# Gate products of a routed expert layer: float32, or split into a rounded part and a rest

## The reference

```
eidx = take_along_axis(cidx, pos)                 # which experts, 8 heads x 16
gate = softmax(top_sc)                            # and their gates
act  = gelu(einsum('thkd,td->thk', u_tab[eb], hb))
y    = einsum('thk,thkd->td', gb * act, v_tab[eb])
```

## Time and profile before

| | us |
|---|---|
| median of 3 runs | 3418.14 (3417.44 to 3432.96) |
| the profiled execution | 3415.01 |
| its span in the profile | 3413.2 |
| PE busy | 3213.3 (94%) |
| DVE busy | 2236.4 (66%) |
| POOL busy | 1723.1 (50%) |
| ACT busy | 1360.5 (40%) |

### The profile page before, as it was taken

The page is one execution under the profiler, slowest core; times in us unless marked ns, Lnnn a source line. Parts: engine busy times, 40 slices in busy tenths (PEclk is TensorE's granted clock), DMA queues, the critical chain, the costliest instruction groups (busy, mean ns, idle before and its releaser), DMA issues.

```text
span 3413.2 us, 46478 instructions
## 1 busy us (share of the span) xinstructions
PE 3213.3 (94%) x16195; PEld 2774.4 (81%) x16195; DVE 2236.4 (66%) x4113; ACT 1360.5 (40%) x1999; POOL 1723.1 (50%) x922
## 2 busy tenths in 40 slices
PE   6999999989999999979999999898999999899998
PEld 4787787779999999979999998756888886478886
DVE  5787898769968677646666645286854332857553
ACT  4555432333454544434444443365322223632221
POOL 2222343434767667657787754662444443034443
PEclk8999999999999999989999999999999999999999
DMA  5434422223689797999999953211222232122222
GB/s 208 156 119 162 150 93 80 93 86 112 209 294 333 249 338 247 325 346 337 343 350 356 335 181 108 85 54 48 94 98 99 95 107 102 48 68 99 98 94 87
DMA packets 190046, 587.55 MB, mean 172 GB/s; under 512 B 19585, under 2 KB 52737, under 8 KB 189601
## 3 DMA queue, kind: packets, MB, share of 16 engines
q1 hardware_dynamic: 83936, 303.08, 25.5%
q10 hardware_dynamic: 69092, 148.25, 12.0%
q0 software_dynamic: 36864, 134.23, 11.8%
HBM read 532.92 MB, written 67.24 MB: 176 GB/s over the span
## 4 chain that ended last, share of the span: by engine, by line
PE 66%; DVE 13%; DMA 8%; issue 5%; ACT 3%; POOL 3%; ACTq 0%; DVEq 0%; SPq 0%; POOLq 0%
PE ps L417 19%; PE ps L419 19%; PE ps L418 19%; DMA ring<-panels 6%; POOL ring_r L2201 3%; PE ps L653 2%; DMA arena<-u_rows,arena 2%; PE ps L781 2%; DVE ps L1781 1%; PE ps L516 1%; ACT high_w L894 1%; PE ps L770 1%; DMA arena<-v_rows,arena 1%; DVE arena L1849 1%; DVE arena L1846 1%
## 5 line engine op out<-in xcount | busy, mean ns | idle before, releaser
L2201 POOL TENSOR_TENSOR ring_r<-ring,high_w 128x1024 fp32r<-128x1024 f32 x552 | 1365.6, 2476 | 1446.1 <-ACT high_w L894 1443.9
L417 PE MATMUL ps<-uT_r,high_w 128*128 128x512 f32 (+1 forms) x2608 | 986.2, 378 | 17.1 <-POOL ring_r L2201 11.5
L419 PE MATMUL ps<-uT_r,ring_r 128*128 128x512 f32 (+1 forms) x2608 | 963.6, 369 | 0.0
L894 ACT ACTIVATE high_w<-ring 128x1024 fp32r<-128x1024 f32 x552 | 582.2, 1057 | 888.1 <-PE ps L419 645.6
L418 PE MATMUL ps<-sq_r,high_w 128*128 128x512 f32 (+1 forms) x2032 | 737.3, 363 | 0.0
L418 PE MATMUL ps<-part,high_w 128*128 128x384 f32 (+1 forms) x1840 | 664.2, 361 | 0.0
L417 PE MATMUL ps<-part,high_w 128*128 128x384 f32 (+1 forms) x1664 | 599.9, 361 | 35.8 <-POOL ring_r L2201 17.3
L419 PE MATMUL ps<-part,ring_r 128*128 128x384 f32 (+1 forms) x1664 | 595.4, 358 | 0.0
L417 PEld LDWEIGHTS ps<-uT_r,high_w 128*128 128x128 f32 x2608 | 493.6, 189 | 89.3 <-POOL ring_r L2201 14.4
L419 PEld LDWEIGHTS ps<-uT_r,ring_r 128*128 128x128 f32 x2608 | 492.7, 189 | 63.4
L418 PEld LDWEIGHTS ps<-sq_r,high_w 128*128 128x128 f32 x2032 | 384.1, 189 | 39.1 <-issue 1.0
(11 more groups left out here) (354 smaller groups left out, 4065.9 us busy)
## 6 DMA issues: line engine op xcount, KB each, us to landing
ring<-panels SPq DMA_DIRECT2D x568, 512.0 KB, 3.4
gdram<-arena ACTq DMA_DIRECT2D x48, 512.0 KB, 7.3
arena<-adram ACTq DMA_DIRECT2D x128, 192.0 KB, 4.8
arena<-gdram ACTq DMA_DIRECT2D x14, 1536.0 KB, 16.8
adram<-arena ACTq DMA_DIRECT2D x102, 192.0 KB, 5.2
arena<-ada_rest ACTq DMA_DIRECT2D x32, 512.0 KB, 4.6
strips_dram<-btab ACTq DMA_DIRECT2D x4, 3584.0 KB
arena<-strips_dram ACTq DMA_DIRECT2D x24, 448.0 KB, 3.4
```

The lines of the kernel that those rows point to most:

```text
L417: t_.matmul(out, wh, xh[:, 0:n], start=(k == 0), stop=False)
L419: last = t_.matmul(out, wl, xh[:, 0:n], start=False, stop=(k == KT - 1))
L894: s_.activation(high_w[:, j % RING], ring[:, j % RING], ACT.Copy).then_inc(hi_ready, 1)
L2201: g_.tensor_tensor(ring_r[:, j], ring[:, j], high_w[:, j], ALU.subtract).then_inc(lo_ready, 1)
```

## The change

The gates are split into a rounded part and the rest, and both operands of the gate products are kept in the rounded format. For each token there are two gated one-hot matrices, one with the rounded gate and one with the rest of it, and PE adds two products of 128 columns in place of one float32 product.

- `gated_a` holds two matrices for each of 8 tokens (`s` is 0 or 1) and takes all of `st`; `is_b` moves into the part of `arena` behind 24064 (`rest_r`), where it now lies inside `cand`, beside `gate_top` and `gate_rest`.
- `one_hots` copies the gates from PSUM into `gate_top` (which rounds them) and subtracts that from them into `gate_rest`. Each gated matrix is then made by a `tensor_scalar` with two scalars per partition, both read from on-chip memory, in place of a `scalar_tensor_tensor` that read the gate from PSUM. There are eight of them to a set, not four.
- `hot_ready` counts 9 to a set, not 5.
- `route(o)` for o of 2 and 3 waits until the last gate product of the stage before it is out, since `cand` now covers operands of it. `gather_v` waits for the last product before the first gather, not before the third.

```
-                    last = t_.matmul(ps[:, 7, k * P:(k + 1) * P], is_b[:, token, :], gated_a[:, token, :], start=True, stop=True)
+                    for s in range(2):
+                        last = t_.matmul(ps[:, 7, k * P:(k + 1) * P], is_b[:, token, :], gated_a[:, token, s, :],
+                                         start=(s == 0), stop=(s == 1))
...
                 if o >= 2:
-                    ve.wait_ge(hot_ready, 5 * 32 * (o - 1))
+                    ve.wait_ge(hot_ready, 9 * 32 * (o - 1))
+                    ve.wait_ge(gmm_done, 32 * (o - 1) + 2)
...
                 ve.wait_ge(slot_tr, o)
-                S.done(v_.tensor_copy(slot_a, ps[:, 4, 0:P]))
+                S.mark(v_.tensor_copy(slot_a, ps[:, 4, 0:P]))
+                S.done(v_.tensor_copy(gate_top, ps[:, 4, 2 * P:3 * P]))
+                S.done(v_.tensor_tensor(gate_rest, ps[:, 4, 2 * P:3 * P], gate_top.bitcast(F32), ALU.subtract))
...
-                        v_.scalar_tensor_tensor(out=gated_a[:, 4 * (n % 2) + k], in0=iota, scalar=slot_a[:, now:now + 1],
-                                                in1=ps[:, 4, 2 * P + now:2 * P + now + 1].broadcast_to([P, P]),
-                                                op0=ALU.is_equal, op1=ALU.mult).then_inc(hot_ready, 1)
+                        for s, gate in enumerate((gate_top.bitcast(F32), gate_rest)):
+                            v_.tensor_scalar(gated_a[:, 4 * (n % 2) + k, s], iota, slot_a[:, now:now + 1], gate[:, now:now + 1],
+                                             ALU.is_equal, ALU.mult).then_inc(hot_ready, 1)
...
                 if k == 0:
                     po.wait_ge(u_done, SLOTS)
-                    po.wait_ge(hot_ready, 5 * 32 * DENSE_TILES)
-                if k == 2:
+                    po.wait_ge(hot_ready, 9 * 32 * DENSE_TILES)
                     po.wait_ge(gmm_done, 32 * DENSE_TILES + 2)
```

More of the change, by code:

```diff
@@ L156, in build @@
         sq, sq_r = both("sq", [P, KT, T])
-        st = sb("st", [P, 4, T])
+        st, st_r = both("st", [P, 4, T])
         ms, sr, rt, rstd = (st[:, n, :] for n in range(4))
@@ L164, in build @@
         part_x = sb("part_x", [P, KT, T], F32R)
-        sb("rest", [P, 27520 - 19968 - KT * T])
+        rest_r = sb("rest", [P, 27520 - 19968 - KT * T], F32R)
         cst = sb("cst", [P, 2 * P])
@@ L223, in build @@
         st_f = st[:].rearrange("p a b -> p (a b)")
-        is_b = st_f[:, 0:8 * P].rearrange("p (a c) -> p a c", c=P)
-        gated_a = st_f[:, 8 * P:16 * P].rearrange("p (a c) -> p a c", c=P)
+        gated_a = st_r[:].rearrange("p a b -> p (a b)").rearrange("p (a s c) -> p a s c", s=2, c=P)
+        is_b = rest_r[:, 25600 - 24064:26624 - 24064].rearrange("p (a c) -> p a c", c=P)
+        gate_top = rest_r[:, 24832 - 24064:24960 - 24064]
         ranked = view(24576, TT, 16, TOPK)
@@ L230, in build @@
         oneh = cand
-        slot_a = cand[:, 0:P]
+        slot_a, gate_rest = cand[:, 0:P], cand[:, P:2 * P]
         u_buf = [view(2048 + D * n, D) for n in range(U_BUFS)]
@@ L647, in hot @@
             def hot(n, par):
-                pe.wait_ge(hot_ready, n * 5 + 5)
+                pe.wait_ge(hot_ready, n * 9 + 9)
                 pe.wait_ge(g_evac, n + 1)
@@ L1255, in _ @@
                 if n == 8 * GROUPS - 2:
-                    act.wait_ge(hot_ready, 5 * 32 * DENSE_TILES)
+                    act.wait_ge(hot_ready, 9 * 32 * DENSE_TILES)
                     for m in range(2):
```

## The result

| | before | after |
|---|---|---|
| median, range | 3417.79 us (3410.29 to 3432.96, 4 runs) | 3485.01 us (3481.68 to 3490.98, 4 runs) |
| ratio | | 1.0206, 95% interval 1.0186 to 1.0225 |
| profiled execution, span | 3415.01, 3413.2 us | 3490.98, 3489.2 us |
| gate groups, first record to last, three stages | 133.5 + 131.9 + 131.4 us | 154.0 + 152.7 + 160.1 us |
| interval from group to group | 4.24 us | 4.99 us |

The account below looks back on a forecast made before the run. PE was taken to bound the stages, DVE having about 40 us of air in the first. 3415.0 us + 110 for DVE's waits + 2 for small edits = 3527, with 3.1 for the median 3530 us; range 3416 to 3600.

Parts of the forecast that it names:

- port case: Three stages: DVE's all-SBUF tensor_scalar waits for POOL, interval 4.24 to 5.42 us, +110 us, time 3530 us; chance 0.57.
- PE's group: Eight rounded products on PE cost 0.91 us a group by their loads (upper end, taken) or 0.46 (lower); before, 0.89.
- rival 3: On PE, short rounded products take four passes: interval 4.24 + 0.89 us, +83 us, 3500 us; chance 0.08.
- DVE's run: Eight tensor_scalar a set at 0.353 us each, 0.265 apart: 2.12 us, 1.09 more than before.
- Rival 1: DVE's tensor_scalar in one-element form, no waiting for POOL: set 4.56 us, +30 us, 3450 us; chance 0.13.
- wait W: DVE's wait for POOL a set, W = (h/P)(2.12 + W) with P = 4.08 + W: 1.34 us.
- hold h: POOL's hold on DVE a set: 2.1 us, subtractions and a quarter of the gathers; bounds 1.80 and 2.93.
- The threshold: DVE's time per set: nothing happens up to 4.24 us; above it every 0.1 us costs 9.3 us.
- The added waits: route(o)'s wait for the last gate product and the v gather's earlier product wait cost nothing.
- The small edits: Two more short DVE instructions at each stage's start (gate_top, gate_rest): +2 us in all.
- The signs: Profile after: single tensor_scalar over 2 us, interval near 5.4, PE waiting over 25 us, u-row waits shrinking, POOL instructions longer.
- rival 4: Second scalar free, no POOL hold, DVE's set 3.57 us, rounded group 0.46: interval 3.81, -40 us, 3378 us; chance 0.10.

Follow-up runs that it names:

- e2: Changed kernel, rest of the gates in PSUM and the eight gated matrices made by scalar_tensor_tensor reading gates from PSUM; 3431.96 us, ratio 1.0053.
- e5: e2 with each token's two gated matrices streamed in one product of 256 columns, parts not summed; 3425.65 us, ratio 1.0028.
- e1: Changed kernel with iota copied into PSUM once a stage and read there by the eight tensor_scalar; 3453.66 us, ratio 1.0105.
- e7: Kernel before, float32 products kept, gates copied into SBUF and its four gated matrices made by two-scalar tensor_scalar; 3451.17 us, ratio 1.0106.
- e10: e7 with iota read from PSUM instead of SBUF; 3420.08 us, ratio 1.0018 against the kernel before.
- e13: Kernel before with only the change's two added waits, route's and the first v gather's; 3415.31 us, ratio 0.9992.
- e6: e2 without the rest of the gates: rounded gates alone, four scalar_tensor_tensor and four rounded products a set; 3402.22 us, ratio 0.9960.

## Why the prediction was right, point by point

- **Where it plays: right.** The profiled executions differ by 76.0 us, and 70.0 of these lie in the three stages, 93 intervals of +0.75 us. Forecast were 3530 us and a port case of 3506 to 3586 (3509 to 3589 with the 3.1 us that its sum adds for the median); 3485.01 is inside the whole range given and 21 us below the port case's own, so it is the width kept for the rivals that holds it.
- **PE's group: right.** The upper end was taken, 0.91 us, from the one-column records of rows 5; it was 0.84 (e2). Four passes, rival 3, are refuted (e5).
- **DVE's run: right.** 0.353 us each and 0.265 apart were expected, 0.335 and 0.257 came: 2.06 us for 2.12. Rival 1 had them 0.327 apart with no holds; both are refuted. The scalar_tensor_tensor that was removed has the same duration (e2, 0.339), so at 128 columns the new form had nothing to give even without the port.
- **The port: right in its mechanism, too large in size.** Instructions over 2 us, equal durations as soon as one operand is in PSUM (e1, e2), and e7 against e10 show it. The formula gave a wait W = 1.34 us a set; 0.98 was measured, 0.36 x 93 = 33 us of the 45 that the forecast was too high. The step that was mis-sized is the hold h: a quarter of the gathers was counted in, and gathers hardly held L1939 (358 met one alone, none over 0.55 us). With the subtractions alone and a run of 2.06 the formula gives 1.11. The rest of the gap is the formula itself: it makes W grow with the length of the run, and the holds were 0.98 with four instructions and with eight. Why they are equal is open.
- **The rest of the 45 us:** the shorter run is 0.06 x 93 = 6, and 1 is in the roundings of the interval. Some 5 remain: the profiled execution after lies 6 above the median of its kernel where before's lay 3 below, which makes 9, and against it the executions differ by 76.0 us of which 70.0 are in the intervals, so 6 outside them where 2 were expected. What those 6 are is not shown.
- **The threshold: wrong.** "Up to 4.24 us nothing happens" took DVE's work a set against the interval. e2 at 4.02 lost 13 to 18 us and e7 at 2.99 + 0.98 = 3.97 lost 32 to 36. DVE's air was not free, not even before, where 99.4 us busy and 38.8 of waits for rows make 138.2 of 141: in it lie the waits for the gathered rows, which come at their own times, 0.34 us a set in e2 and 14.0/32 = 0.44 in e7. 4.02 + 0.34 = 4.36 and 3.97 + 0.44 = 4.41 come near the measured 4.41 and 4.55. The change itself went so far past the threshold (5.00) that the waits had gone to 1.5 us, so the error did not show there.
- **The added waits: right.** Nothing (e13). The small edits of one_hots were not run by themselves.
- **The signs: mostly right.** Single instructions over 2 us came, and DVE's waits for rows shrank. The interval is 4.99 and not near 5.4, and PE's wait for the line in the first stage is 21.7 us and not over 25, both as the smaller hold has it. POOL's subtractions did not get longer (median 2400 ns after, 2401 before).
- **The gain on the other side (rival 4):** its cheap product of 0.058 us did not come (0.105 in e2, 0.10 in e6), and splitting float32 in two rounded products saves PE 0.05 us a group. Even half the products gives 10 to 14 us of 46 (e6) while the gathers stand where they are.

The Trainium skill (SBUF — State Buffer, SBUF: two separate sides) had the mechanism: an exclusive lock for the whole instruction. By its words the gathers would hold the port as well, and the prediction's upper end rested on that beside its rows; here 358 instructions of L1939 met a gather and no subtraction, and none took over 0.55 us. For gathers the measurement decides. Its figure for a load of 128 columns, 107 ns (TensorE: Matmul & The Clock Gate, LDWEIGHTS), agrees with the 0.105 us a product; the 81 ns of its Back-to-back issue gap was not reached in any run here.

## What to carry to other kernels

Before an instruction is swapped for a "cheaper" one, look where its operands lie: with everything in SBUF it waited here for the neighbouring engine's long instructions, and one operand in PSUM, though 0.07 us dearer each, was 31 us cheaper in sum. Add up an engine's set with its waits for data, not its work alone, before calling the rest of the interval air. Cutting the neighbour's long instruction in two does not help a run of such instructions: one passes between the halves and the next waits for the second. And splitting a float32 product in two rounded ones paid nothing on PE at 128 columns (0.84 us a group for 0.89), where a product's time isn't set by its columns.

## What the runs showed of the hardware

- A rounded product of 128 columns with its own load takes 0.105 us, one of 256 columns 0.14; a float32 one of 128 columns is two records 0.11 us apart.
- An indirect gather on POOL hardly held a DVE instruction that lies in SBUF alone: 358 of them met one and took 0.55 us at most. A subtraction of 2.40 us did hold it, to its end.
- The holds were about 1 us a set with four and with eight such instructions, and did not shrink when POOL's instruction was halved: DVE got in one instruction between the halves, and the second half held the next (97 holds for 63).
- tensor_scalar with two scalars and 128 columns: 0.335 us from SBUF, 0.402 from PSUM.
- After idle time PE's products ran at half pace. In the change PE was idle for 3.21 us until 1077.72 us, waiting for L1939, and then had a granted clock of 0.50 (the 1.2 GHz level) until about 1084 us, busy all the time. The chain after, in order of time, shows 0.32 us for a product there and 0.17 us from 1084.5 on; the granted clock of the three stages was 0.96, 0.97 and 0.94 where it had been 0.99, 1.00 and 0.99. DVE was the late one, so this is not added to the loss; no run separates the two.

```profile
1078.00:1084.00 6.00, 6.00 (x22) 6.00 (x22) 6.00 (x19) 1.43 (x2) 0.00 (x0) 0.50 0.30 87
```

```profile
1077.72 1.97 PE ps L655 x8
...
1083.95 0.32 PE ps L419
...
1084.48 0.17 PE ps L418
...
1085.01 0.84 PE ps L655 x8
```
